# Asking for three modulation sums later in the first projections of a two-block transformer kernel, and spreading their tiles of products in another pattern

## The reference, cut to what matters

```
cond_x = silu(c);  cond_c = silu(c_ctx)
for i in (0, 1):
    sx1, cx1, gx1, sx2, cx2, gx2 = split(cond_x @ ada_w[i] + ada_b[i], 6)
    sc1, cc1, gc1, sc2, cc2, gc2 = split(cond_c @ ada_w[i] + ada_b[i], 6)
    hx = rms(x) * (1 + cx1) + sx1
    ...
    u = hx @ w_in                       # in layer 0, also for the context
    a_x, a_c, a_b, f = split(u, 4)
    a_y = a_b * conv3(a_c * a_x)
    f_y = real(fft over tokens and over groups of 64 channels of f)
    x = x + gx1 * (concat(a_y, f_y) @ w_out)
    x = x + gx2 * mlp(rms(x) * (1 + cx2) + sx2)
```

## Time and profile before

| what | value |
|---|---|
| median of 3 runs | 2317.66 us (2316.68 to 2317.85) |
| the profiled execution's own time | 2320.05 us |
| its span in the trace | 2318.3 us |
| PE busy | 2149.3 us, 93% |
| DVE busy | 1218.6 us, 53% |
| ACT, POOL busy | 786.0 us, 34%; 675.3 us, 29% |
| the chain that ended last | PE 82%, DVE 8%, POOL 3%, issue 3%, ACT 2%, DMA 1% |
| mean granted clock of PE | 0.961 of full |

### The profile page before, as it was taken

One profiled execution on the slowest core, in us unless ns is written; L12 is line 12 of the kernel. 1 busy time (PEld: TensorE's weight loads), 2 busy tenths in 40 slices (PEclk: granted clock), 3 DMA queues, 4 the chain that ended last, 5 costly groups with the idle time before them and its releaser, 6 DMA issues.

```text
span 2318.3 us, 33033 instructions
## 1 busy us (share of the span) xinstructions
PE 2149.3 (93%) x13426; PEld 1839.4 (79%) x13426; DVE 1218.6 (53%) x1594; ACT 786.0 (34%) x1267; POOL 675.3 (29%) x314
## 2 busy tenths in 40 slices
PE   5898989999999997999899999999999896999987
PEld 3687878888888885889777888888998695977766
DVE  3787658455565446560873322223788315066652
ACT  2212223122222124332873333222323533355542
POOL 0331313222222222222893444444021124200002
PEclk9998989999999999999999999999998897999998
DMA  7333324224332231221322333333221011211110
GB/s 282 125 128 117 121 72 138 99 84 151 100 127 90 94 100 45 72 60 46 56 45 80 103 95 93 94 96 91 73 83 55 10 55 45 75 55 56 55 46 36
DMA packets 74953, 199.92 MB, mean 86 GB/s; under 512 B 25296, under 2 KB 26576, under 8 KB 74832
## 3 DMA queue, kind: packets, MB, share of 16 engines
q1 hardware_dynamic: 73648, 197.60, 27.6%
q10 hardware_dynamic: 1184, 0.61, 0.1%
HBM read 194.51 MB, written 2.10 MB: 85 GB/s over the span
## 4 chain that ended last, share of the span: by engine, by line
PE 82%; DVE 8%; POOL 3%; issue 3%; ACT 2%; DMA 1%; SPq 0%; DVEq 0%; ACTq 0%
PE ps L2044 59%; PE ps L2159 5%; PE ps L2516 5%; PE ps L2059 3%; POOL NAP L856 2%; DVE ada_acc L1386 1%; PE ps L2069 1%; PE ps L2083 1%; PE ps L2220 1%; DMA ring<-stream 1%; PE ps L2540 1%; PE ps L2076 1%; DVE S L1454 1%; PE ps L2552 1%; DVE UC L1751 1%
## 5 line engine op out<-in xcount | busy, mean ns | idle before, releaser
L809 POOL TENSOR_TENSOR WL<-raw,WH 128x1024 fp32r<-128x1024 f32 x215 | 523.7, 2439 | 1349.7 <-ACT WH L906 1349.4
L906 ACT ACTIVATE WH<-raw 128x1024 fp32r<-128x1024 f32 x260 | 273.2, 1054 | 499.6 <-PE ps L2044 471.9
L2044 PE MATMUL ps<-HH,WH 128*128 128x512 f32 (+2 forms) x1568 | 423.8, 336 | 2.5 <-DVE HL L1853 2.5
L2044 PE MATMUL ps<-HH,WL 128*128 128x512 f32 (+2 forms) x1568 | 418.4, 333 | 0.0
L2044 PE MATMUL ps<-HL,WH 128*128 128x512 f32 (+2 forms) x1568 | 418.0, 333 | 0.0
L2044 PEld LDWEIGHTS ps<-HH,WH 128*128 128x128 f32 x1568 | 252.0, 188 | 37.6 <-issue 3.6
L2044 PEld LDWEIGHTS ps<-HL,WH 128*128 128x128 f32 x1568 | 251.6, 188 | 34.0 <-issue 1.4
L2044 PEld LDWEIGHTS ps<-HH,WL 128*128 128x128 f32 x1568 | 251.2, 188 | 31.2
L2044 PE MATMUL ps<-GH,WH 128*128 128x512 f32 (+1 forms) x896 | 266.0, 355 | 3.0 <-issue 3.0
L2044 PE MATMUL ps<-GH,WL 128*128 128x512 f32 (+1 forms) x896 | 266.6, 355 | 0.0
L2044 PE MATMUL ps<-GL,WH 128*128 128x512 f32 (+1 forms) x896 | 265.4, 354 | 0.0
(11 more groups left out here) (269 smaller groups left out, 3384.7 us busy)
## 6 DMA issues: line engine op xcount, KB each, us to landing
raw<-stream SPq DMA_DIRECT2D x260, 512.0 KB, 3.6
ring<-stream SPq DMA_DIRECT2D x80, 512.0 KB, 3.7
ADA<-stream SPq DMA_DIRECT2D x4, 2048.0 KB, 20.8
XT<-rpb SPq DMA_DIRECT2D x128, 24.0 KB, 2.4
XT<-xT SPq DMA_DIRECT2D x1, 2048.0 KB, 8.7
out<-XT SPq DMA_DIRECT2D x8, 256.0 KB, 2.0
V1s<-V SPq DMA_DIRECT2D x6, 256.0 KB, 4.6
XT<-ctxT SPq DMA_DIRECT2D x1, 1024.0 KB, 11.2
```

What stands on the lines that cost most here:

```text
L809: nc.gpsimd.tensor_tensor(WL[:, slot, :], raw[:, slot, :], WH[:, slot, :].bitcast(F32), ALU.subtract).then_inc(lo_done[slot], 1)
L906: nc.scalar.activation(WH[:, slot, :], raw[:, slot, :], ACT.Copy).then_inc(hi_done[slot], 1)
L2044: ins = nc.tensor.matmul(pair(g)[:, cols], lhs, x[:, k, cols], start=first, stop=last)
```

## The change

```
-IN1_ADA = {1: 2, 2: 2, 3: 2, 4: 2, 5: 1, 6: 2, 7: 2, 8: 1, 9: 2, 11: 1, 12: 2, 13: 3, 14: 1, 15: 1}
-IN1_SUMS, IN1_TURNS = {4: 0, 11: 1}, {5: 0, 12: 1}
+IN1_ADA = {1: 2, 2: 2, 3: 2, 4: 2, 7: 3, 8: 1, 9: 2, 10: 2, 11: 2, 12: 2, 13: 3, 14: 1}
+IN1_SUMS, IN1_TURNS = {6: 0, 11: 1}, {8: 0, 13: 1}
...
     for t in range(6):
         g(("dft1", t))
-        if t == 0:
+        if t == 3:
             sums(0, 2)
...
-                if i in IN1_TURNS:
-                    ada_cols(0, IN1_TURNS[i])
+                if i in IN1_SUMS:
+                    sums_out(0, IN1_SUMS[i])
                 if i == 1:
                     dve.wait_ge(silu_done, 1)
                 products_beside(("in1", i))
-                if i in (4, 10):
-                    sums_out(0, i // 10)
+                if i in IN1_TURNS:
+                    ada_cols(0, IN1_TURNS[i])
...
-                if t == 0:
+                if t == 3:
                     sums_out(0, 2)
...
-                if t == 0:
+                if t == 3:
                     ada_sums(0, 2)
```

## The result

| | before | changed |
|---|---|---|
| median | 2317.42 us (4 runs, 2316.68 to 2317.85) | 2302.26 us (4 runs, 2299.31 to 2303.48) |
| ratio, 95% interval | | 0.9934 (0.9918 to 0.9949) |
| a second set, median | 2317.70 us (9 runs) | 2298.72 us (5 runs, 2296.94 to 2302.04) |
| its ratio | | 0.9923 (0.9909 to 0.9936) |
| profiled execution, span | 2320.05, 2318.3 us | 2299.31, 2297.5 us |

The change makes the kernel faster, by 15.2 us in the first set and 19.0 in the second. 2301.2 was forecast.

What follows compares the result with a forecast made beforehand. PE, busy 93% of the span, was taken to bound the kernel. Gains of 10.7 us before group 15 ends, less 1.0, plus 6.8 in the Fourier step gave 16.5: 2317.66 becomes 2301.2 us, range 2297.0 to 2306.5.

Steps and rivals of the forecast that it cites:

- First stall and restart: PE's 9.1 us wait at the sums of b = 0 and 1.6 us half-clock restart go: 10.7 us gained.
- The sums of b = 1: PE asks for them at 156.7 us; a new wait of 1.0 us, bounds 0 and 1.8.
- Group 15: PE's last projection would end at 193.3 us, the new wait of 1.0 us included; 202.96 before.
- DVE's pace: DVE is done with the projections at 201 us (steps: 200.7 to 202.9) and sets the Fourier step, not PE.
- The Fourier step: Between group 15's end and `dft2`: 6.8 us gained, with `dft2` starting at 211.0 instead of 227.56.
- the second stall: PE's 7.72 us idle before the sums of b = 2; those sums would no longer be held by DVE's products.
- The waits of 1 to 2 us between groups of `dft1`: Sign that the forecast holds: PE waits there, released by DVE's line 1604, not 1386.
- The meetings with POOL: Eight DVE products beside one POOL split take 7.53 us instead of 5.3; each meeting costs 2.2 us.
- The first: Rival: PE sets the pace to the end, DVE keeps up; gain 20.9 us, 2296.8; chance 0.12.
- The second and third: Rivals: DVE falls 5 us further behind, 2306.2, chance 0.10; stall at b = 2 returns, 2308.9, chance 0.06.
- The fourth: Rival: DVE's total work up to the Fourier step counts; under 4.6 us change, 2313 to 2320; chance 0.04.
- The fifth: Rival: a projection's weights come late behind ring loads, PE stands; slower, 2319 and up; chance 0.02.

Runs made afterwards that it cites:

- first_sums_back: Changed kernel with only the sums of b = 0 put back behind group 4; 2308.76 us, one run; group 4's copy to `dft2` 124.1 us.
- only_pattern: Changed kernel with sums of b = 0 back behind group 4 and of b = 2 back behind dft1 t = 0; 2311.05 us, one run.
- no_splits: Changed kernel with POOL's remainder cut to 8 of 1024 columns for weight tiles of groups 9 to 15 and Fourier matrices; 2296.45 us, one run.
- pad_group5: Changed kernel with two extra writes of zeros on DVE behind group 5's convolution; 2304.74 us, one run.

## Why the prediction was right

**First stall and restart: right.** 10.7 us were forecast, first_sums_back shows 10.5. In the changed kernel the sums run in 1.00 us, without a wait.

**The sums of b = 1: right.** A new wait of 1.0 us was taken, 1.21 measured.

**Group 15.** From the copy of group 4 it took 106.93 us to `dft1` before and takes 97.69 now (191.10 - 93.41), 9.2 us less. 9.7 were forecast.

**DVE's pace: right in kind, 1.4 us too slow.** Its remainder of group 15 ends at 196.9, which is 199.5 on the clock of the kernel before (2.6 us added for the earlier start). 201 was taken, with 200.7 to 202.9 from the steps. Group 14's step took 4.7 us (186.76 to 191.41) where 6.1 was charged, since it met only the end of a split: its first convolution instruction took 1.45 us, 0.8 over the 0.65 without a split, on top of the 3.9 named for that case. Group 11's step took 5.1 (155.26 to 160.35) for the same 6.1. `dft2` starts at 209.6 on that clock, against 211.0. This is the difference between 16.5 and 17.9.

**The Fourier step: 1.9 us more than forecast, and its parts not priced.** 6.8 us were forecast, 8.7 came (24.6 to 15.9 us from `dft1` to `dft2`). The prediction let the sums' later place and DVE's earlier end work together and did not price them apart. It counted both of DVE's long waits, 15.4 us, towards that earlier end. The runs do tell the parts apart. The later place gives 1.1 us here, 2.8 alone. The first of the two waits, 8.63 us, moves DVE and PE alike and does nothing for the second stall: only_pattern still has it (8.63), and the stall is 1.37 us. What mended the stall is the pattern, which filled the 6.77 us and left group 15 without a tile. The waits of 1 to 2 us between groups of `dft1` that were named as a sign are 0.98 us in all.

**The meetings with POOL.** 2.2 us were charged for one, 2.1 measured between the changed kernel and no_splits. The reading of the row held up: in the changed kernel, too, the first of the eight products began 0.1 us ahead of the split (168.59 against 168.70), and the eight lost the 2.1 us all the same.

**The rivals.** The first was the nearest. PE's pace gives 20.4 us, and the change reaches 17.9 of it. What was said against it was loose: a split begins 1.2 us (117.34 against 116.11) to 2.9 us (128.38 against 125.45) behind the end of PE's group, not with it. The second and third did not come. The fourth is refuted: in place of DVE's 15.4 us of long waits for PE there are 4.5. One of the two stood at sums that do not move (b = 1); it went because DVE's copy of them moved and tiles stand ahead of it. The fifth did not arise; no wait of a projection for a split is listed.

**The time.** 2301.2 was forecast and 2302.26 measured, closer than the terms deserve, which is luck: they were 1.4 us off in the stretch, and the start and what lies behind `dft2` scatter by more. The second set has 2298.72. One part of the scatter is the start, 3.2 us between the earliest and the latest copy of group 4. Another lies behind `dft2`: from there to the end it took 2090.7 us before, 2090.5 in the first profile of the changed kernel, 2086.8 in the second and 2093.7 in pad_group5, with the same instructions.

## What to carry to other kernels

When an in-order PE asks for another engine's result, ask as late as the result allows: two groups later cost nothing here and gave 10.5 of 17.9 us, half-clock restart included. Do not take a second stall further on for an echo of the first: while PE stood, the feeding engine waited as long, and the two kept step. Here the second stall came from seven tiles of work left behind the feeding engine's last wait, and with one of them moved ahead and none behind the last group the stall was 1.4 us instead of 7.7, with the first stall in place. So undo the parts one by one before crediting a move. And measure such a change between two marks in the trace, where it repeated to 0.1 us in two profiles, while the time of the whole kernel scattered by 4 to 5 us.

## What was not expected of the hardware

**The start differs from run to run.** The same instructions end group 4 anywhere from 93.4 to 96.6 us. Twelve small matmuls of the first norm (line 2083) took 2.93 us in the profile before and 1.60 in the changed kernel's:

```profile
32.24 2.93 PE L2083 MATMUL ps<-con,small 128*128 128x128 f32 x12 [0.91 <-DVE small L1460]
```

```profile
31.86 1.60 PE L2083 MATMUL ps<-con,small 128*128 128x128 f32 x12 [0.92 <-DVE small L1460]
```

The granted clock is given as 1.00 from 32 to 36 us in both, so this row's cause stays open. It is 1.60 in the four of the fourteen profiles with the earliest copy of group 4 (93.41 to 94.80) and 2.93 in the ten others (95.25 to 96.61). From 40 to 47 us the clock does differ, 0.53 before and 0.76 here:

```profile
40.00:47.00 7.00, 4.61 (x20) 3.41 (x24) 6.62 (x12) 3.29 (x6) 0.00 (x0) 0.53 0.28 111
```

```profile
40.00:47.00 7.00, 6.92 (x35) 4.38 (x36) 5.59 (x11) 3.23 (x6) 0.00 (x0) 0.76 0.25 99
```

**Writes of zeros pass a split.** A write of 128 x 1024 zeros on DVE took 0.91 us beside a split of POOL and 0.91 without one, where one of the products takes 0.74 us at the least and 2.96 at the most in the changed kernel. The Trainium skill (SBUF — State Buffer, Who interferes with whom) says that a DVE instruction with at most one SBUF input, outside the 2-port modes, does not contend with GpSimd. The rows agree for a write without an input; whether it ran outside those modes they do not show. So what DVE does during a split need not be lost, if it is of that kind.
